# Gate table built for eight tokens at a time: one-hot tiles by broadcast compares, scaled by VectorE and ScalarE, and twelve expert tiles in a search round

## The reference, cut to what matters

```
q  = (h2 @ peer_wq).reshape(bsz, seq, 8, 256)
s1 = einsum('bshd,hnd->bshn', q[..., :128], peer_k1);  s2 = the same with the other half and peer_k2
v1, i1 = top_k(s1, 16);  v2, i2 = top_k(s2, 16)
sc, ci = top_k(v1[..., :, None] + v2[..., None, :], 16)      # over the 256 pairs
experts = i1[ci // 16] * 128 + i2[ci % 16]                    # 128 of 16384 experts per token
gates = softmax(sc)
z  = einsum('td,tkd->tk', h, peer_u[experts])
y2 = einsum('tk,tkd->td', gelu(z) * gates, peer_v[experts])
```

## Time and profile before

| what | value |
|---|---|
| median of three runs | 4066.32 us |
| the profiled execution | 4060.72 us |
| its span | 4059.4 us |
| PE busy | 3650.7 us, 90% |
| DVE busy | 2122.4 us, 52% |
| ACT busy | 1421.4 us, 35% |
| POOL busy | 1485.3 us, 37% |
| mean granted clock of PE | 0.949 |

### The profile page before, as it was taken

How to read it: one execution, slowest core, us unless ns; L and a number is a source line. 1 busy time by engine, 2 the same in 40 slices (tenths; PEclk the granted TensorE clock), 3 DMA queues, 4 the chain that set the end, 5 groups by cost and what they waited for, 6 DMA issues and landing times.

```text
span 4059.4 us, 50035 instructions
## 1 busy us (share of the span) xinstructions
PE 3650.7 (90%) x19310; PEld 2966.7 (73%) x19310; DVE 2122.4 (52%) x4445; ACT 1421.4 (35%) x2076; POOL 1485.3 (37%) x724
## 2 busy tenths in 40 slices
PE   4986889999999899979885798789999999999998
PEld 4875667887767578857773487668878888888885
DVE  2265446555445374245767329999973332323334
ACT  3544433334334332234323332234433323322232
POOL 5742224444223234333210143222234454454452
PEclk8998999999999999989876899899999999999999
DMA  4520114443212134222000123335563544445441
GB/s 158 176 76 32 63 52 156 135 146 104 71 55 94 51 117 133 93 73 81 27 2 21 52 94 117 96 117 184 205 213 128 166 145 145 156 137 164 140 157 56
DMA packets 298042, 445.39 MB, mean 110 GB/s; under 512 B 8144, under 2 KB 219088, under 8 KB 295760
## 3 DMA queue, kind: packets, MB, share of 16 engines
q1 hardware_dynamic: 278640, 371.22, 28.0%
q0 software_dynamic: 19168, 70.98, 5.4%
HBM read 383.45 MB, written 58.72 MB: 109 GB/s over the span
## 4 chain that ended last, share of the span: by engine, by line
PE 74%; DVE 16%; ACT 4%; issue 3%; POOL 1%; DMA 1%; DVEq 0%; POOLq 0%; ACTq 0%; SPq 0%
PE bank L438 21%; PE bank L440 20%; PE bank L439 20%; PE bank L2576 3%; PE bank L519 2%; DVE arena_rw L2110 2%; POOL split_low L424 1%; DVE arena L2657 1%; PE bank L1629 1%; PE bank L1653 1%; DVE arena L2659 1%; DVE arena L2663 1%; PE bank L1287 1%; PE bank L1914 1%; DVE arena L2661 1%
## 5 line engine op out<-in xcount | busy, mean ns | idle before, releaser
L424 POOL TENSOR_TENSOR split_low<-weights,split_high 128x1024 fp32r<-128x1024 f32 x554 | 1343.7, 2432 | 2219.1 <-ACT split_high L416 2211.0
L438 PE MATMUL bank<-normed_high,split_high 128*128 128x512 f32 x2480 | 990.2, 399 | 76.1 <-issue 38.8
L439 PE MATMUL bank<-normed_low,split_high 128*128 128x512 f32 x2480 | 974.6, 393 | 0.0
L440 PE MATMUL bank<-normed_high,split_low 128*128 128x512 f32 x2480 | 974.1, 393 | 0.0
L416 ACT CAST split_high<-weights 128x1024 fp32r<-128x1024 f32 x554 | 574.4, 1047 | 677.1 <-PE bank L440 577.0
L438 PEld LDWEIGHTS bank<-normed_high,split_high 128*128 128x128 f32 x2480 | 472.1, 190 | 185.8 <-issue 52.8
L438 PE MATMUL bank<-hidden_high,split_high 128*128 128x512 f32 x1536 | 600.9, 391 | 7.2 <-ACT hidden_high L2652 4.8
L440 PE MATMUL bank<-hidden_high,split_low 128*128 128x512 f32 x1536 | 599.1, 390 | 0.0
L439 PE MATMUL bank<-hidden_low,split_high 128*128 128x512 f32 x1536 | 599.0, 390 | 0.0
L439 PEld LDWEIGHTS bank<-normed_low,split_high 128*128 128x128 f32 x2480 | 472.6, 191 | 99.1 <-issue 3.1
L440 PEld LDWEIGHTS bank<-normed_high,split_low 128*128 128x128 f32 x2480 | 471.2, 190 | 100.8
(11 more groups left out here) (385 smaller groups left out, 4254.8 us busy)
## 6 DMA issues: line engine op xcount, KB each, us to landing
weights<-in_w_ff SPq DMA_DIRECT2D x64, 1024.0 KB, 5.4
weights<-in_peer_u SPq DMA_DIRECT2D x64, 1024.0 KB, 5.9
weights<-in_peer_v SPq DMA_DIRECT2D x64, 1024.0 KB, 5.0
gate_table<-arena SPq DMA_DIRECT2D x16, 2048.0 KB, 7.7
gates<-gate_table POOLq DMA_DIRECT2D x32, 1024.0 KB, 9.8
weights<-in_cond_w SPq DMA_DIRECT2D x24, 1024.0 KB, 5.3
early_table<-branch SPq DMA_DIRECT2D x72, 256.0 KB, 2.1
lates<-early_table POOLq DMA_DIRECT2D x18, 1024.0 KB, 11.2
```

The lines of the kernel that those rows point to most:

```text
L424: pool.do.tensor_tensor(lo, raw_unit(u), hi.bitcast(F32), ALU.subtract).then_inc(*pool.sig("split_low", u))
L438: pe.do.matmul(o, ah, bh, start=first, stop=False)
L439: pe.do.matmul(o, ah, bl, start=False, stop=False)
L440: return pe.do.matmul(o, al, bh, start=False, stop=last)
```

## The change

Eight tokens make one step. A ring buffer holds both one-hot tiles of eight tokens, (side, token, key), and there are three of them, in the same memory as the 24 single ones. DVE makes the eight tiles of a side with one `tensor_tensor` compare of 128 x 1024: the counter repeated over the tokens against the key repeated along the row. The gates are no longer part of the compare. DVE multiplies the first four tokens' tiles by the gates with a third `tensor_tensor` (128 x 512), and ACT scales the other four with four activations of 128 x 128 whose scale is a column of gates. ACT scales group m before it copies the banks of group m - 1. PE works through the eight tokens in two halves, and the second half also waits for ACT.

The early tiles are divided otherwise: 12 in a search round (4 before the scores and 8 after), 48 in all, and 24 in the table, after groups 1, 4 and 6 of each eight. SP's and POOL's counts follow.

```
-SCORES_AHEAD = 4
+HOT = 8
+SEARCH_TILES = 12
...
-        hots = Ring([arena(8192 + j * 256, 256) for j in range(24)], marks)
+        hots = Ring([arena(8192 + j * 2048, 2048).rearrange("p (s t n) -> p s t n", s=2, t=HOT) for j in range(3)], marks)
...
+        def early_with(m):
+            return m % 8 in (1, 4, 6)
...  (PE and ACT, in each search round)
-                fill(ahead, 6)
+                fill(ahead, SEARCH_TILES - 4)
...  (PE, table)
+            for m in range(N_HOT):
+                hot = hots.tile(m)
+                for half in range(2):
+                    n = 2 * m + half
+                    bank, empty = banks.take("gate", n)
+                    pe.wait_ge(empty, at("hot_scaled", m), at("hot_scaled_act", m) if half else None)
+                    for j in range(4):
+                        t = 4 * half + j
+                        last = pe.do.matmul(bank[:, j * P:(j + 1) * P], hot[:, 0, t, :], hot[:, 1, t, :],
+                                            start=True, stop=True)
+                    last.then_inc(*pe.sig("gate", n))
+                    banks.give(("gate", n), ("gate_staged", n))
+                if early_with(m):
                     fill(ahead)
...  (ACT, table)
+            for m in range(N_HOT + 1):
+                if m < N_HOT:
+                    act.wait_ge(at("hot", m))
+                    for t in range(4, HOT):
+                        key1 = hots.tile(m)[:, 1, t, :]
+                        act.do.activation(key1, key1, ACT.Identity, scale=turned3[:, 2, HOT * m + t:HOT * m + t + 1]
+                                          ).then_inc(*act.sig("hot_scaled_act", m))
+                for n in (2 * m - 2, 2 * m - 1) if m else ():
+                    block, t4 = staged_at(n)
+                    act.wait_ge(at("gate", n), table_written(block - 2) if block > 1 else None)
+                    act.do.copy(stages[block % 2][:, :, t4:t4 + 4], banks.tile("gate", n)
+                                .rearrange("p (t a) -> p a t", t=4)).then_inc(*act.sig("gate_staged", n))
+                if m and early_with(m - 1):
                     fill(ahead)
...  (DVE, table)
+            numbers = counter.unsqueeze(1).to_broadcast([P, HOT, P])
+            for m in range(N_HOT):
+                hot, empty = hots.take(m)
                 dve.wait_ge(empty)
+                side = [turned3[:, k, HOT * m:HOT * (m + 1)].unsqueeze(2).to_broadcast([P, HOT, P]) for k in range(3)]
+                dve.do.tensor_tensor(hot[:, 1], numbers, side[0], ALU.is_equal).then_inc(*dve.sig("hot", m))
+                dve.do.tensor_tensor(hot[:, 0], numbers, side[1], ALU.is_equal).then_inc(*dve.sig("dve_step"))
+                dve.wait_ge(at("hot", m))
+                dve.do.tensor_tensor(hot[:, 1, 0:4], hot[:, 1, 0:4], side[2][:, 0:4], ALU.mult
+                                     ).then_inc(*dve.sig("hot_scaled", m))
+                hots.give((m,), ("gate", 2 * m + 1))
...  (SP, table)
-            fill(ahead, TT * 10)
+            fill(ahead, TT * SEARCH_TILES)
             for block in range(N_BLOCKS):
-                fill(ahead, 2)
+                fill(ahead, 1 + block % 2)
```

More of the change, by code:

```diff
@@ L2496, in build, with staged_at @@
         N_BLOCKS = T // STAGE_TOKENS
-        BATCHES = T // 4
+        N_HOT = T // HOT
+        def early_with(m):
+            return m % 8 in (1, 4, 6)
+        def staged_at(n):
+            return n // (STAGE_TOKENS // 4), 4 * (n % (STAGE_TOKENS // 4))
         n_early = EARLY_GROUPS * GROUP
@@ L2671, in dve_peer @@
             meet(dve, "dve", "gates")
-            for t in range(T):
-                hot, empty = hots.take(t)
+            numbers = counter.unsqueeze(1).to_broadcast([P, HOT, P])
+            for m in range(N_HOT):
+                hot, empty = hots.take(m)
                 dve.wait_ge(empty)
[L2675 to L2679, removed]
+                side = [turned3[:, k, HOT * m:HOT * (m + 1)].unsqueeze(2).to_broadcast([P, HOT, P]) for k in range(3)]
[5 more added lines that the diff above has]
+                hots.give((m,), ("gate", 2 * m + 1))
             meet(dve, "dve", "experts")
@@ L2772, in pool_peer @@
                 pool.do.dma_start(keys[j], dram[f"peer_k{j + 1}"]).then_inc(*pool.land("peer_keys_landed", j))
-            pool_split(early_unit(TT * 10 - 1) + AHEAD)
+            pool_split(early_unit(TT * SEARCH_TILES - 1) + AHEAD)
             meet(pool, "pool", "gates")
```

## The result

The changed kernel takes 4017.84 us in the median of four runs (4016.0 to 4019.27), against 4066.29 before (four runs as well, three when the forecast was made): a ratio of 0.9883, 95% interval 0.9869 to 0.9897, 48.4 us less. The forecast was 4022, 43.7 less. The profiled execution took 4018.33 us (span 4017.0) against 4060.72, which is 42.4 less. The difference between the two figures lies upstream of the change: the stages that nobody touched ended 5.5 us later in this execution than in the one of before.

The account below looks back on a forecast made before the run. The prediction took DVE to pace the old table and PE the new one. Table -54.1 us and search +10.4 turned the profiled 4060.7 into 4017.0; with 5.6 for the median, 4022.6, forecast as 4022, range 4009 to 4045.

Parts of the forecast that it names:

- DVE paced the old table and PE the new one: Table: DVE held PE back by 0.4 us per 16 tokens; afterwards PE is the bound, DVE 1.0 us under it.
- PE's work of 244.8 us: Table: PE needs 30.6 us for eight steps with three expert tiles, eight times over.
- the lower clock and waits of 4.5: Table: +1.5 us for PE at 1.2 GHz after a longer rest, +3 for in-order ACT waits and the ring.
- a start 2.3 later: Table: the first step is ready after 3.0 us, where the first token took 0.7.
- Prices: Table, length of the new instructions: 1024-element compare 1.22 us, 512-element multiply 0.68, activation 0.40 and 0.31 apart.
- The slower rival: Table: POOL catches every wide compare, 2.8 us each, 448 us for the stage, 4220 in all; chance 0.04.
- ACT just in time: Table: ACT's scaling barely meets PE's need in runs of three steps after a tile, 4.4 us against 4.36.
- Each subtraction takes 2.2 us from DVE: Table: each POOL subtraction costs DVE 2.2 us, 3 x 2.2 in eight steps.
- the full ring: Table: during a tile DVE soon has all three buffers full and would rest anyway, so the subtractions' losses fall there.
- The search 10.4 us longer: Search: two more subtractions a round cost DVE 0.5 and 2.1 us, 2.6 in each of four rounds; bounds 3 and 14.
- Nothing for the DMAs and for the end of the table: Table: no time taken for SP's DMAs, nor for the last staged bank replacing the last tile before the meeting.
- The median 5.6 us above the profiled execution: Whole kernel: the median of the runs lies 5.6 us above the profiled execution, added to 4017.0 to give 4022.6.

Follow-up runs that it names:

- the two parts alone: Two kernels: the kernel before with only the tiles divided anew, 4052.9 us; the changed kernel with the old division of the tiles, 4051.7 us.
- the second one: The changed kernel measured again, unaltered: 4019.3 us, 0.9886 of the kernel before.
- ACT scales all: The changed kernel with ACT scaling all eight tiles by the gates and DVE none: 4057.3 us.
- the table only: The changed kernel with the old division of the tiles, 10 in a search round and 32 in the table: 4051.7 us.
- DVE scales all: The changed kernel with DVE multiplying all eight tiles by the gates in one 128x1024 instruction and ACT none: 4043.0 us.
- The run without subtractions: The kernel in which DVE multiplies all eight tiles, with POOL's 24 subtractions of the table cut to 8 elements: 4018.9 us.
- late casts: The changed kernel, where ACT casts two units of each search round only after the exponential: 4018.2 us.
- the thirteenth tile: The changed kernel with 13 tiles in each search round and 20 in the table: 3998.3 us, 0.9846 of the kernel before.

## Why the prediction was right, and where its sizes were off

- *DVE paced the old table and PE the new one.* Right, and shown from both sides by the two parts alone (DVE: 284 expected for 24 tiles, 285.9 measured; PE: 296 expected for 32 tiles, 289 of it work, 294 measured).
- *PE's work of 244.8 us, the lower clock and waits of 4.5, and a start 2.3 later.* Measured 249.1 and 2.5. The sum of -54.1 came out at -54.1 in the profiled execution and at -53.8 in the second one. The mechanism is right; that it fits to a tenth is luck. The lower clock cost 2.5 us and not 1.5: the first 32 gate matmuls took 6.24 us where 3.73 is their full-speed length, most of them 0.21 us apart and not 0.11. The waits cost 249.1 - 244.8 - 2.5 = 1.8 us and not 3.
- *Prices.* Compare 1.22 long (forecast 1.22), multiply 0.68 (0.68), activation 0.396 with four in 1.28 us, so 0.30 apart (0.40 and 0.31). All were read from neighbours of the same form. The slower rival, a compare of 1.6 us or more, had no ground: the longest was 1.23.
- *ACT just in time.* Right for the changed kernel (PE waited for it once, 0.6 us) and shown to be a real margin by the run in which ACT scales all.
- *Each subtraction takes 2.2 us from DVE.* This was mis-sized for the table: 15.4 us over 24 of them, 0.64 each. The prediction had the loss hidden by the full ring. The trace shows that for 17 of 24 it does not arise: POOL lets DVE pass and works while DVE waits for a buffer. It did no harm to the sum, since PE was the bound either way. It is no rule: with the table only, 29 of 31 cost the full 2.2 us, though DVE waited 30 us for PE there, and where DVE scales all, each cost 1.5. The Trainium skill (SBUF, State Buffer, section "SBUF: two separate sides") gives the pair of ports to whichever instruction starts first; the prices here agree with that (2.2 us of a 2.4 us subtraction). The run without subtractions shows that nothing else made that table long.
- *The search 10.4 us longer.* This is the term that was off: +6.7, and +8.9 in the second measurement of the same kernel. The second figure is the usual one: in the four other kernels with twelve tiles and no late casts the search took 302.9 or 303.0 us, 8.8 more than before. So 1.6 us of the miss are the forecast's, and 2.1 belong to one execution. Rounds 0 and 1 grew by 2.5 and 2.9 us (2.6 forecast). Round 2 grew by 1.2: the subtraction that used to fall on DVE's shift (L2731, 1.30 us in that round before) now misses it (L2752, 0.38). Round 3 did not grow in the profiled execution (72.6 against 72.7) and grew by 2.3 in the other. In both its old losses are gone: the eight additions (L2743) took 2.78 us and not 4.97, the shift (L2752) 0.23 and not 2.06. In the first, two new ones took their place, one in each group of multiplies (4.85 and 4.98). In the other there were three, two in the first group (7.03) and one in the compare behind it (4.53). The forecast had one hit and one compare held back there. It held the old losses fixed and added the new ones, but tiles that shift the phase of POOL's work move all of them.
- *Nothing for the DMAs and for the end of the table.* Right: the rest is 0.3 us shorter.
- *The median 5.6 us above the profiled execution.* The forecast carried this offset over to the changed kernel, where it did not recur (4017.8 against 4018.3). The execution of before had its untouched stages 5.5 us faster than that of the changed kernel, which makes up most of the offset: it says nothing of the change. Between the medians 48.4 us were measured and 43.7 forecast; table and search together give 47.4 in the profiled execution and 44.9 in the second.

## What to carry to other kernels

Where two engines are within a few per cent of each other, relieve both in one step: here either part alone gave about a quarter of the gain (12 and 14 us, 48 together). Price the bound of a stage from the same instruction at a place where nothing holds it (32 matmuls in 3.49 us, not 3.90). When a long idle wait is left in front of a hand-over, put work into it that the hand-over does not need, and look at which other engine's work comes with it: the tile was free for PE, and its subtraction was not free for DVE.

## What was not expected of the hardware

- The exclusion between DVE's two-input instructions and POOL's subtraction works both ways, and back-to-back DVE instructions can pass a waiting POOL instruction more than once. In the table of the changed kernel a subtraction of 2.40 us lasted 4.65 in the median (2.397 to 5.204), while in the old table, with single compares of 0.27 us, POOL was hardly made to wait (2.40 in the median, 2.64 at most) and DVE lost 2.2 us each time. With DVE all but gapless, one subtraction lasted 25.6 us.
- The trace does not say what decides between the two. In the changed kernel all subtractions that came due 0.14 us into L2696 got in behind it, and those that came due 0.53 us into L2695 let that one and two more pass. But where DVE scales all, of two that came due 0.49 us into L2689 one got in behind it (at 2758.49) and the other waited for 21 to end (at 2770.92). That was not settled.
- With the thirteenth tile PE was busy without a gap through rounds 1 and 2 of the search, and the granted clock there was 1.00 (the 2.4 GHz level), where it was 0.92 and 0.89 in the kernel before, which rested 12.6 us in front of each of these rounds and started them at the 1.2 GHz level.
